# Attention products of a hybrid decoder step: full-precision products against three products of high and low halves

## The reference, cut to what matters

```
z = rmsnorm(x, g_mix) @ w_in;  u, q, k, v, ga, gb = split(z)
pooled = windowed means of u (window 2, 4, 8, 16 by group) - u
pool_out = (pooled @ w_pool[group]) * pool_scale
# retention, chunks of 128 rows, 4 heads, keys 128 wide, values 256 wide
scores = (q_c @ k_c.T) * dmask
o      = scores @ v_c + (q_c @ s) * xi
s      = g_chunk * s + (k_c * zeta).T @ v_c
ret_out = head_group_norm(o) * ret_gn
x += (sigmoid(ga) * pool_out + sigmoid(gb) * ret_out) @ w_out
x += hier_moe(rmsnorm(x));  y = rmsnorm(x)
```

## Time and profile before

| what | value |
|---|---|
| median of 3 runs | 1019.6 us (1019.0 to 1019.87) |
| the profiled execution | 1017.89 us, of which its span is 1016.2 us |
| PE busy | 966.5 us, 95% of the span |
| weight loads (PEld) busy | 837.1 us, 82% |
| DVE busy | 745.7 us, 73% |
| ACT / POOL busy | 441.6 us / 234.3 us |
| chain that ended last, by engine | PE 85%, DVE 6%, DMA 4% |

### The profile page before, as it was taken

One profiled execution on the slowest core, in us unless ns is written; L12 is line 12 of the kernel. 1 busy time (PEld: TensorE's weight loads), 2 busy tenths in 40 slices (PEclk: granted clock), 3 DMA queues, 4 the chain that ended last, 5 costly groups with the idle time before them and its releaser, 6 DMA issues.

```text
span 1016.2 us, 16180 instructions
## 1 busy us (share of the span) xinstructions
PE 966.5 (95%) x5356; PEld 837.1 (82%) x5357; DVE 745.7 (73%) x1648; ACT 441.6 (43%) x736; POOL 234.3 (23%) x239
## 2 busy tenths in 40 slices
PE   6999999999999999999999999969999999999980
PEld 6998888988889888898886888858888888888870
DVE  4975566855578455684558755589999999999985
ACT  6622122121221111301113122138888988988964
POOL 0001220012200112001221110032444434433333
PEclk9999999999999999999999999979999999999995
DMA  9511105121051210511117442289999999999975
GB/s 315 182 42 54 34 30 174 32 64 32 32 173 32 63 32 26 179 32 53 63 46 254 168 163 88 105 311 411 395 389 394 398 394 387 396 392 385 365 259 203
DMA packets 76259, 191.79 MB, mean 189 GB/s; under 512 B 13887, under 2 KB 48811, under 8 KB 63763
## 3 DMA queue, kind: packets, MB, share of 16 engines
q1 hardware_dynamic: 60971, 159.07, 41.4%
q0 software_dynamic: 15072, 31.27, 10.1%
q10 hardware_dynamic: 144, 0.52, 0.2%
HBM read 173.75 MB, written 38.68 MB: 209 GB/s over the span
## 4 chain that ended last, share of the span: by engine, by line
PE 85%; DVE 6%; DMA 4%; issue 2%; ACT 2%; POOL 1%; SPq 0%; DVEq 0%; POOLq 0%; ACTq 0%
PE bank L2128 18%; PE bank L906 11%; PE bank L908 11%; PE bank L907 11%; PE bank L2129 9%; PE bank L937 8%; PE bank L1077 3%; PE bank L2117 1%; PE bank L977 1%; DMA raw<-in_w_in_dram 1%; PE bank L2143 1%; PE bank L2151 1%; PE bank L2139 1%; PE bank L2147 1%; DMA sample_state<-in_state_ret_dram 1%
## 5 line engine op out<-in xcount | busy, mean ns | idle before, releaser
L1367 DVE TENSOR_TENSOR w_lo<-w,w_hi 128x1024 fp32r<-128x1024 f32 x128 | 150.4, 1216 | 0.3
L799 ACT ACTIVATE w_hi<-w 128x1024 fp32r<-128x1024 f32 x128 | 129.4, 1068 | 2.8 <-PE bank L908 2.8
L906 PE MATMUL bank<-w_hi,xT_hi 128*128 128x512 f32 x256 | 102.9, 402 | 1.9 <-issue 1.7
L2128 PE MATMUL bank<-wvg_hi,hT_hi 128*128 128x512 f32 x256 | 104.4, 408 | 0.0
L2483 POOL TENSOR_TENSOR mixed<-onorm,pgate 128x256 f32<-128x256 f32 x36 | 38.9, 1081 | 272.8 <-DVE onorm L2299 272.8
L2128 PE MATMUL bank<-wvg_lo,hT_hi 128*128 128x512 f32 x256 | 100.9, 394 | 0.0
L2128 PE MATMUL bank<-wvg_hi,hT_lo 128*128 128x512 f32 x256 | 100.7, 393 | 0.0
L908 PE MATMUL bank<-w_hi,xT_lo 128*128 128x512 f32 x256 | 100.3, 392 | 0.0
L907 PE MATMUL bank<-w_lo,xT_hi 128*128 128x512 f32 x256 | 99.7, 390 | 0.0
L1935 ACT ACTIVATE v<-bank 128x256 f32<-128x256 f32 x32 | 12.3, 383 | 201.3 <-PE bank L2129 201.3
L906 PE MATMUL bank<-hT_hi,wuqk_hi 128*128 128x344 f32 x288 | 94.1, 327 | 0.1
(11 more groups left out here) (293 smaller groups left out, 2416.6 us busy)
## 6 DMA issues: line engine op xcount, KB each, us to landing
w<-in_w_dram SPq DMA_DIRECT2D x96, 1024.0 KB, 17.6
raw<-in_w_in_dram SPq DMA_DIRECT2D x57, 256.0 KB, 3.4
mixed_d<-mixed POOLq DMA_DIRECT2D x32, 128.0 KB, 2.2
sample_state<-in_state_ret_dram SPq DMA_DIRECT2D x16, 256.0 KB, 3.8
out_dram<-sample_state SPq DMA_DIRECT2D x16, 256.0 KB, 3.7
mixed_in<-mixed_d SPq DMA_DIRECT2D x8, 512.0 KB, 4.3
x_again<-in_x_prompt_dram SPq DMA_DIRECT2D x8, 512.0 KB, 3.5
h_d<-h POOLq DMA_DIRECT2D x8, 512.0 KB, 3.0
```

The source lines that it names most:

```text
L799: act.activation(hi, whole_w, ACT.Copy).then_inc(S["up_hi"], 1)
L906: pe.matmul(out, lhs[0], rhs[0], start=first, stop=False)
L1367: dve.tensor_tensor(lo, whole_w, hi, ALU.subtract).then_inc(S["up_lo"], 1)
L2128: g = pe.matmul(gates, x[xi], wvg[wi][:, 1:3, k, :], start=first, stop=last)
```

## The change

- The products L2139 (pooled rows), L2143 (scores) and L2151 (keys) become `three` products of F32R halves each. The product with the state, L2147, stays. In the last head the pooled rows stay one float32 product.
- ACT now writes `kz` and `v` as F32R (high halves). DVE makes the low halves `kz_lo` and `v_lo` from the same PSUM banks, splits the masked scores into `scm` and `scm_lo` (three instructions in place of one), splits `wp` (three in place of one, heads 0 to 2) and the pooled line (`pool_halves`, two instructions of 1024 columns, heads 0 to 2).
- The sample rows' pooled product (L2017) becomes two float32 products in heads 0 to 2.
- `before(c)` waits for `scm_done` ahead of its transpose; `attend(0)` waits for scores(1), not only scores(0); `pool_ready` comes behind `pool_halves`.
- The norm weights are loaded by head, 256 at a time, as a fourth load of `pool_loads`, behind two more waits (`so_mm`, `sgn_done`); the one load of 1024 goes.

```diff
-        gn_b = rb.place("gn_b", [P, D], F32)
+        gn_b = rb.place("gn_b", [P, DV], F32)
+        v_lo = rb.place("v_lo", [P, DV], F32R)
+        kz_lo = [rb.place(f"kz_lo{i}", [P, P], F32R) for i in range(2)]
+        scm_lo = [rb.place(f"scm_lo{i}", [P, P], F32R) for i in range(2)]
...
-            sp.dma_start(gn_b[:, :], ret_gn[0:1, :].to_broadcast([P, D])).then_inc(gains_in, 16)
...
+                    sp.wait_ge(S["so_mm"], after(4 * h - 3))
+                    carried(sp, "sp")
+                    sp.wait_ge(S["sgn_done"], after(9 * h))
+                    carried(sp, "sp")
...
-                sp.dma_start(ps_b[:, :], pool_scale[0:1, bass.ds(h * DV, DV)].to_broadcast([P, DV]))\
-                    .then_inc(misc_in, 16)
+                for row, dst in ((pool_scale, ps_b), (ret_gn, gn_b)):
+                    sp.dma_start(dst[:, :], row[0:1, bass.ds(h * DV, DV)].to_broadcast([P, DV])).then_inc(misc_in, 16)
...
-                        pe.matmul(sample_bank(h)[Q3:P, DV:2 * DV], ps32[:, :], wp[:, :], start=True, stop=True)
+                        if h == H - 1:
+                            pe.matmul(pooled, ps32[:, :], wp[:, :], start=True, stop=True)
+                        else:
+                            pe.matmul(pooled, ps32[:, :], wp_hi[:, :].bitcast(F32), start=True, stop=False)
+                            pe.matmul(pooled, ps32[:, :], wp_lo[:, :].bitcast(F32), start=False, stop=True)
...
                 def before(c):
                     pe.wait_ge(S["kz_ev"], after(9 * h + c))
+                    pe.wait_ge(S["scm_done"], after(8 * h + c))
...
-                    pe.wait_ge(S["scm_done"], after(8 * h + c))
                     pe.matmul(banks[5][:, 0:P], kT[:, at:at + P], qT[:, at:at + P], start=True, stop=True)\
...
-                    pe.matmul(banks[6][:, DV:2 * DV], line[1][:, HIST + c * P:HIST + (c + 1) * P], wp[:, :],
-                              start=True, stop=True)
-                    pe.wait_ge(S["scm_done"], after(8 * h + c + 1))
+                    if h == H - 1:
+                        pe.matmul(banks[6][:, DV:2 * DV], line[1][:, at], wp[:, :], start=True, stop=True)
+                    else:
+                        three(pe, banks[6][:, DV:2 * DV], [line_hi[:, at], line_lo[:, at]],
+                              [wp_hi[:, :], wp_lo[:, :]], True, True)
+                    pe.wait_ge(S["scm_done"], after(8 * h + c + 1 + (c == 0)))
...
-                    o = pe.matmul(banks[6][:, 0:DV], scm[s][:, :], vb[s][:, :], start=True, stop=(c == 0))
+                    values = [vb[s][:, :], v_lo[:, :]]
+                    o = three(pe, banks[6][:, 0:DV], [scm[s][:, :], scm_lo[s][:, :]], values, True, c == 0)
...
-                    pe.matmul(banks[7][:, 0:DV], kz[s][:, :], vb[s][:, :], start=True, stop=True)\
+                    three(pe, banks[7][:, 0:DV], [kz[s][:, :], kz_lo[s][:, :]], values, True, True)\
...
-                dve.tensor_tensor(wp[:, :], wp_raw[:, :], ps_b[:, :], ALU.mult).then_inc(S["wp_ready"], 1)
+                if last:
+                    dve.tensor_tensor(wp[:, :], wp_raw[:, :], ps_b[:, :], ALU.mult).then_inc(S["wp_ready"], 1)
+                else:
+                    steps.do(dve.tensor_tensor(ps_b[:, :], wp_raw[:, :], ps_b[:, :], ALU.mult))
+                    steps.do(dve.tensor_copy(wp_hi[:, :], ps_b[:, :]))
+                    dve.tensor_tensor(wp_lo[:, :], ps_b[:, :], wp_hi[:, :], ALU.subtract).then_inc(S["wp_ready"], 1)
+
+                def low_k(c):
+                    dve.wait_ge(S["kz_ev"], after(9 * h + c + 1))
+                    dve.scalar_tensor_tensor(out=kz_lo[c % 2][:, :], in0=banks[4][:, 0:P], scalar=head_col(0),
+                                             in1=kz[c % 2][:, :], op0=ALU.mult, op1=ALU.subtract)
+
+                def low_v(c):
+                    dve.wait_ge(S["v_ev"], after(9 * h + c + 1))
+                    dve.tensor_tensor(v_lo[:, :], banks[2 + c % 2][:, 0:DV], vb[c % 2][:, :], ALU.subtract)
...
-                    dve.tensor_tensor(scm[c % 2][:, :], banks[5][:, 0:P], head_tab(h, 0, P), ALU.mult)\
+                    steps.do(dve.tensor_tensor(scores_f[s][:, :], banks[5][:, 0:P], head_tab(h, 0, P), ALU.mult))
+                    steps.do(dve.tensor_copy(scm[s][:, :], scores_f[s][:, :]))
+                    dve.tensor_tensor(scm_lo[s][:, :], scores_f[s][:, :], scm[s][:, :], ALU.subtract)\
                         .then_inc(S["scm_done"], 1)
...
+                def pool_halves():
+                    at = slice(HIST, HIST + SEQ)
+                    dve.wait_ge(S["ut_mm"], after(h + 1))
+                    steps.do(dve.tensor_copy(line_hi[:, at], line[1][:, at]))
+                    dve.tensor_tensor(line_lo[:, at], line[1][:, at], line_hi[:, at], ALU.subtract)\
+                        .then_inc(S["pool_ready"], 1)
...
                     if c < CH:
+                        low_k(c)
                         scores(c)
...
                         grow_state(c - 1)
+                        if c < CH:
+                            low_v(c)
...
+                    if c == 0:
+                        low_v(0)
+                        if not last:
+                            pool_halves()
```

More of the change, by code:

```diff
@@ L223, in step_kernel @@
         hc = rb.place("hc", [P, H, HCW], F32)
-        gn_b = rb.place("gn_b", [P, D], F32)
+        gn_b = rb.place("gn_b", [P, DV], F32)
+        v_lo = rb.place("v_lo", [P, DV], F32R)
+        kz_lo = [rb.place(f"kz_lo{i}", [P, P], F32R) for i in range(2)]
+        scm_lo = [rb.place(f"scm_lo{i}", [P, P], F32R) for i in range(2)]
+        scores_f = [nc.alloc_sbuf_tensor_at(f"scores{i}", [P, P], F32, offset=rb.where[f"scm_lo{i}"]) for i in range(2)]
         line = [rb.place(f"line{i}", [P, SPAN + 1], F32) for i in range(3)]
@@ L234, in step_kernel @@
         ps_b = rb.place("ps_b", [P, DV], F32)
-        vb = [rb.place(f"v{i}", [P, DV], F32) for i in range(2)]
+        vb = [rb.place(f"v{i}", [P, DV], F32R) for i in range(2)]
         sg = [rb.place(f"sg{i}", [P, 2 * DV], F32) for i in range(2)]
         sgn = [t[:, DV:2 * DV] for t in sg]
-        kz = [rb.place(f"kz{i}", [P, P], F32) for i in range(2)]
-        scm = [rb.place(f"scm{i}", [P, P], F32) for i in range(2)]
+        kz = [rb.place(f"kz{i}", [P, P], F32R) for i in range(2)]
+        scm = [rb.place(f"scm{i}", [P, P], F32R) for i in range(2)]
         onorm = rb.place("onorm", [P, DV], F32)
@@ L245, in step_kernel @@
         ps32 = rb.place("ps32", [P, 32], F32)
+        line_hi, line_lo = (nc.alloc_sbuf_tensor_at(f"line_{n}", [P, SPAN + 1], F32R, offset=rb.where[at])
+                            for n, at in (("hi", "line0"), ("lo", "line1")))
+        wp_hi, wp_lo = (nc.alloc_sbuf_tensor_at(f"wp_{n}", [P, DV], F32R, offset=rb.where[at])
+                        for n, at in (("hi", "wp"), ("lo", "ps_b")))
         hist = nc.alloc_sbuf_tensor_at("hist", [P, P], F32, offset=rb.where["scm1"])
@@ L1547, in scale_rows @@
                         .then_inc(S["y_done"], 1)
-            dve.wait_ge(gains_in, 32)
+            dve.wait_ge(gains_in, 16)
             for kind, n in TAIL:
@@ L1890, in head @@
                         act.wait_ge(S["pool_ready"], after(h))
+                        act.wait_ge(S["o_mm"], after(8 * h))
                         act.wait_ge(S["ut_mm"], after(h))
@@ L2016, in attend_samples @@
                             pe.wait_ge(S["o_used"], after(9 * h + 8))
-                        pe.matmul(sample_bank(h)[Q3:P, DV:2 * DV], ps32[:, :], wp[:, :], start=True, stop=True)
+                        pooled = sample_bank(h)[Q3:P, DV:2 * DV]
+                        if h == H - 1:
[3 more added lines that the diff above has]
+                            pe.matmul(pooled, ps32[:, :], wp_lo[:, :].bitcast(F32), start=False, stop=True)
                     read(n - 3)
@@ L2047, in first_products @@
                     if i == 6:
-                        pe.wait_ge(misc_in, 48)
+                        pe.wait_ge(misc_in, 64)
                         pe.transpose(banks[4][:, 0:NB * HIST], hist[0:NB * HIST, :],
@@ L2071, in head @@
                     if n == 7:
-                        pe.wait_ge(misc_in, 48 * h + 48)
+                        pe.wait_ge(misc_in, 64 * h + 64)
                         pe.wait_ge(S["kz_ev"], after(9 * h))
@@ L2084, in before @@
                     pe.wait_ge(S["kz_ev"], after(9 * h + c))
+                    pe.wait_ge(S["scm_done"], after(8 * h + c))
                     at = c * P
                     if c == CH:
-                        pe.wait_ge(S["scm_done"], after(8 * h + 8))
                         pe.transpose(banks[4][:, 0:P], kw[:, :], ident).then_inc(S["kt_mm"], 1)
@@ L2257, in between_qk @@
                         low_first(q)
-            per_head, per_tail = 106, 7 + NEWTON
+            HALVES = 3
+            per_head, per_tail = 125, 7 + NEWTON
             def finish(h, c):
@@ L2385, in pool_means @@
                         op0=ALU.mult, op1=ALU.subtract))
```

(13 more changed lines are left out.)

6 lines of the change are left out of this document (4 added, 2 removed).

## The result

| | median | executions | against before |
|---|---|---|---|
| before | 1018.69 us (1016.64 to 1022.62) | 14 | |
| changed | 1022.27 us (1019.57 to 1025.45) | 14 | 1.003, 95% interval 1.002 to 1.0041 |

The change makes the kernel slower by 0.3%, which is 3.1 us by the ratio (the two medians differ by 3.6). The forecast was 1019.1 us, no measurable change. The profiled execution of the changed kernel took 1020.25 us with a span of 1018.6, 2.4 above that of before.

A forecast was written before the change was run, and what follows sets the result against it. PE, busy for 95% of the span, was taken as the bound. Terms -7.0 + 1.3 + 4.3 + 0.9 = -0.5 us, from 1019.6, gave 1019.1 us; range 1014.8 to 1022.6 us.

The forecast's parts named there:

- Products: PE in the four heads: 88 float32 products become three F32R products each, saving 0.080 us apiece, -7.0 us.
- weight loads would have shown: Rival on PE: 0.19 us weight load added to each short product, 43 us more, 1062 us; chance 0.02.
- Samples' pooled product: PE's sample reads in heads 0 to 2: one more float32 product of 0.43 us each, +1.3 us.
- Head starts: Start of heads 1 to 3: PE waits 1.7, 1.7 and 0.9 us for DVE's scores, +4.3 us.
- attend(0): First attend of a head, now behind scores(1): DVE in time by 1.2 us, so no wait, cost 0.
- The loads: SP's extra load ahead of the sample states' reload: 0.7 us in head 1, 0.1 each in 2 and 3, +0.9 us.
- the reload of the sample states is late: Rival: slow norm-weight load delays the update in heads 1 to 3, 4.4 us instead of 0.9, 1022.6 us; chance 0.12.
- The middle chunks: Middle chunks of a head: DVE's extra 1.2 us a chunk fits in its 4.10 us idle time, cost 0.

The follow-up runs named there:

- e6: Changed kernel with all four pool loads behind the sample states' reload and the pooled rows left in float32: 1018.52 us, 0.9997 of before.
- e4: Changed kernel with kz_lo and scores of chunk 0 of heads 1 to 3 ahead of the pooled means' last steps: 1018.38 us, 1.0 of before.
- e1: Changed kernel with the per-head norm weights' load moved behind the sample states' reload and the last weight pieces: 1018.69 us, 1.0007 of before.
- e2: Changed kernel with all four pool loads moved behind the sample states' reload and the last weight pieces: 1017.54 us, 0.999 of before.
- e3: Kernel before with one DVE instruction of 0.34 us repeated in chunk 7 of heads 0 to 2: 1020.56 us, 1.0026 of before.
- e16: Kernel before with POOL's norm-weight address fixed at columns 0 to 255, no load or wait added: 1020.93 us, 1.0025 of before.
- e17: Kernel before with norm weights loaded by head before the reload, two SP waits, own columns per head, POOL's address from a register: 1022.83 us, 1.0038.
- e12: Changed kernel with norm weights loaded behind the reload and DVE's first three weight-piece halves made before the samples' last normalisation: 1017.04 us, 0.9989 of before.

## Why the prediction was wrong

- **Products**: forecast -7.0, 88 x 0.080. Right; the rows say 0.118 a product. The Trainium skill (FP8 and Floating Point Precision, TensorE Precision Notes) has four passes for full precision, by which they would have saved 9.5; the trace has 0.433 to 0.118, 3.7 to 1. By the Trainium skill (TensorE: Matmul & The Clock Gate, The mechanism) weight loads would have shown; at 0.118 a product with new weights each time none does.
- **Samples' pooled product**: +1.3 forecast, 0.44 each. Right for its own length. e6 shows that PE's arrival at the update changes with it, so it is partly cover for that wait.
- **Head starts**: +4.3 forecast, 4.1 in the profile (1.70, 1.58, 0.80 against 1.7, 1.7, 0.9), 3.1 in time (e4). The step that was least sure was right, and so was attend(0).
- **The loads**: +0.9 forecast. This is the step that failed. In the profile it is 3.8, and edits at this place give back 2.4 (e1) to 4.1 us (e2). I took SP's 0.74 us for one load as the whole delay of the reload, 0.7 us in head 1 and 0.1 in the others. The reload went out 1.6, 1.25 and 0.1 us later, only 0.4 to 0.5 of it by the load's own issue, and the waits grew by 1.8, 0.9 and 1.1. In head 3 the update came 5.2 us after the reload's issue, against 4.0 in e1, where `gn_b` stands behind; the load's 128 KB may be what held it, which is not shown. That the update in heads 2 and 3 was not held by the reload did not make room: in head 3 PE already waited 0.64 us for it. The rival "the reload of the sample states is late" had the place, and I gave it 0.12. That its 1022.6 us is the result but for 0.3 is partly luck: it rests on slow issues on SP, and the changed kernel's profile has none.
- **The middle chunks**, "cost 0": true of them, and misread for the last ones. I asked who waits for `o_used` and did not follow DVE's end of the head to the slots, SP and the reload. 0.34 us there cost 2.6 (e3), by a path that is not traced.
- **Not in the sum at all**: `kblk`'s 0.58 us more in each head, which came with the fixed address on POOL, 2.5 us alone (e16).
- The last three, loads, `v_lo` and `kblk`, share one wait of PE. Alone in the kernel before they cost 3.9 (e17), 2.6 (e3) and 2.5 us (e16); in the changed kernel they came to 3.8 us of waits together, and taking one away gave back most (e1: 2.4). They are not to be added there. How the 3.1 us divide among them stays open.

## What to carry to other kernels

Where a releasing instruction is already held a little, as the update was by 0.12 us, take the whole chain behind it as critical, and follow it back through every queue it crosses: here DVE, the weight slots, SP, DMA, DVE again, PE. Price each edit at each link of that chain, however small. Read the granted clock behind every wait of PE that grows, since the wait may not be its whole cost. And put loads that are due late behind those that are due soon: with the same arithmetic, that and an earlier score turned +3.1 us into -5.5.

## What was unexpected of the hardware

- Two SBUF-heavy instructions on DVE and POOL that start together: 1.23 and 1.81 us, or 1.81 and 0.73, with a few nanoseconds between the two cases; the form of POOL's address moves them (e16), and is not all (e12).
- Eight of the twelve waits of 1.72 to 3.06 us for the update were followed by 3.4 us at half of PE's clock, which is 1.7 us of PE's time more, by the estimate above.
- The cast of 128 columns to F32R takes 0.23 us alone and 0.68 beside POOL's sum; in the middle chunks that is hidden:

```profile
102.33 0.73 POOL L2538 TENSOR_TENSOR mixed<-onorm,pgate 128x256 f32<-128x256 f32 x1 [5.23 <-DVE onorm L2320]
102.47 0.68 DVE L2401 CAST scm<-scores 128x128 fp32r<-128x128 f32 x1
```

- An issue on SP of 0.34 to 0.52 us takes 0.95 to 1.83 now and then: 15 of the 219 small loads of heads 1 to 3, all of them in kernels that load in front of the reload. What SP waits for there, no view shows.
